# Prompt attention: the value products of a pair of heads in two column tiles of 64, in batches of two query tiles

## The reference, cut to what matters

```python
o_c = jnp.einsum("bqghc,bcgd->bqghd", p_c.astype(vc.dtype), vc)      # compressed keys
...
o_s = jnp.einsum("bqghm,bqgmd->bqghd", p_s.astype(v_sel.dtype), ...)  # selected blocks
...
o_w = jnp.einsum("bqghw,bwgd->bqghd", p_w.astype(vw.dtype), vw)       # window
...
o = g[..., 0, :] * o_c + g[..., 1, :] * o_s + g[..., 2, :] * o_w
return o.reshape(b, nq, D_ATTN).astype(q.dtype)
```

## Time and profile before

| | before |
|---|---|
| median of 3 runs | 1059.06 us (1058.37 to 1059.9) |
| profiled execution, its own time | 1058.09 us |
| its span, first to last instruction | 1056.0 us |
| TensorE busy | 986.1 us, 93% of the span |
| VectorE busy | 649.7 us, 62% |
| ScalarE busy | 404.6 us, 38% |
| GpSimd busy | 386.6 us, 37% |

### The profile page before, as it was taken

How to read it: one execution, slowest core, us unless ns; L and a number is a source line. 1 busy time by engine, 2 the same in 40 slices (tenths; PEclk the granted TensorE clock), 3 DMA queues, 4 the chain that set the end, 5 groups by cost and what they waited for, 6 DMA issues and landing times.

```text
span 1056.0 us, 19270 instructions
## 1 busy us (share of the span) xinstructions
PE 986.1 (93%) x7168; PEld 836.4 (79%) x7168; DVE 649.7 (62%) x1399; ACT 404.6 (38%) x794; POOL 386.6 (37%) x328
## 2 busy tenths in 40 slices
PE   2999999999999959999899998999699999999996
PEld 0989998998899729998799678999577777756684
DVE  4498999899989679320751312344888888833103
ACT  5333334333334276221331111244577777711001
POOL 2487888788878658001010000000333333100000
PEclk9999999999999959999899999998799999999796
DMA  8243453355334450360255015211630000260002
GB/s 342 75 128 101 127 174 103 101 139 163 101 105 137 139 202 1 120 238 7 115 152 133 1 26 221 80 61 41 205 124 1 0 1 1 104 235 1 1 1 85
DMA packets 43016, 108.01 MB, mean 102 GB/s; under 512 B 20674, under 2 KB 21730, under 8 KB 38530
## 3 DMA queue, kind: packets, MB, share of 16 engines
q1 hardware_dynamic: 42946, 106.99, 31.2%
HBM read 81.87 MB, written 12.17 MB: 89 GB/s over the span
## 4 chain that ended last, share of the span: by engine, by line
PE 82%; DVE 7%; issue 4%; ACT 4%; POOL 3%; DMA 0%; DVEq 0%; ACTq 0%
PE ps L567 52%; PE ps L953 7%; PE ps L593 4%; PE ps L843 4%; POOL C L1737 3%; PE ps L731 2%; PE ps L831 2%; PE ps L939 1%; PE ps L545 1%; DVE SX L1527 1%; DVE KL L1496 1%; PE ps L820 1%; PE ps L795 1%; DVE X L1263 1%; PE ps L822 1%
## 5 line engine op out<-in xcount | busy, mean ns | idle before, releaser
L567 PE MATMUL ps<-Hh,ringAh 128*128 128x256 f32 (+1 forms) x768 | 161.2, 291 | 14.3 <-DVE X L1263 14.3
L567 PE MATMUL ps<-Hh,ringAl 128*128 128x256 f32 (+1 forms) x768 | 159.4, 289 | 0.0
L1307 DVE SCALAR_TENSOR_TENSOR acc<-VP,tapc,acc 128x512 f32<-128x512 f32 x122 | 159.1, 1304 | 0.0
L567 PE MATMUL ps<-Xl,ringAh 128*128 128x256 f32 (+1 forms) x768 | 158.1, 287 | 0.0
L1706 POOL TENSOR_TENSOR ringAl<-ringA,ringAh 128x1024 fp32r<-128x1024 f32 x48 | 121.1, 2535 | 73.3 <-ACT ringAh L1029 73.2
L567 PEld LDWEIGHTS ps<-Hh,ringAh 128*128 128x128 f32 x768 | 123.3, 189 | 27.2 <-DVE X L1263 14.6
L567 PEld LDWEIGHTS ps<-Xl,ringAh 128*128 128x128 f32 x768 | 124.1, 189 | 0.0
L567 PEld LDWEIGHTS ps<-Hh,ringAl 128*128 128x128 f32 x768 | 123.0, 189 | 0.0
L1307 DVE SCALAR_TENSOR_TENSOR ps<-VP,tapc,ps 128x512 f32<-128x512 f32 x138 | 102.8, 745 | 0.6
L843 PE MATMUL ps<-PTB,V 128*128 128x512 f32 (+3 forms) x256 | 91.0, 439 | 2.5 <-ACT PTB L1206 2.1
L567 PE MATMUL ps<-Hh,ringEh 128*128 128x256 f32 (+1 forms) x384 | 84.2, 302 | 7.1 <-DVE ringEl L1373 4.6
(11 more groups left out here) (233 smaller groups left out, 2059.6 us busy)
## 6 DMA issues: line engine op xcount, KB each, us to landing
ringA<-in_w_a SPq DMA_DIRECT2D x16, 1536.0 KB, 7.3
G<-VP SPq DMA_DIRECT2D x60, 260.0 KB, 4.8
ringE<-in_w_f SPq DMA_DIRECT2D x24, 512.0 KB, 3.6
ringC<-in_w_c SPq DMA_DIRECT2D x8, 1024.0 KB, 5.9
cache_cmp<-in_cache_cmp SPq DMA_DIRECT2D x32, 128.0 KB, 2.8
cache_sel<-in_cache_sel SPq DMA_DIRECT2D x16, 256.0 KB, 3.0
cache_win<-in_cache_win SPq DMA_DIRECT2D x1, 4096.0 KB, 15.2
out_win_s<-in_win_state SPq DMA_DIRECT2D x1, 4032.0 KB, 18.1
```

What stands on the lines that cost most here:

```text
L567: mm = nc.tensor.matmul(dst, w, x[:, cols], start=begins, stop=ends)
L1307: nc.vector.scalar_tensor_tensor(tap_sum(k % 2), src, w, tap_sum(k % 2), ALU.mult, ALU.add).then_inc(conv_step, 1)
```

## The change

The order of a step's units becomes: branch b, then early (t = 0, 1) or late (t = 2, 3) query tiles, then head r, then t. So four units in a row hold both heads' weights for two query tiles of one branch. After units 1, 5, 9 and 13 TensorE issues a batch `pv(i, m)` for four such units: for each key tile the products of both heads in turn, each with 64 columns of `V` as the stationary operand, head 0 into rows 0 to 63 and head 1 into rows 64 to 127 of one bank, which alternates with the step. The product of the compressed branch is issued once per step, ahead of the first batch. The transposed weights lie in two tiles, `PTA` for early and `PTB` for late query tiles. The gate product is one instruction over 128 rows. The queries `QS` exist twice and are made a step earlier; the bias is made after the last score that uses the old one. TensorE's loop over steps is written out; VectorE's and GpSimd's loops take two steps in a turn.

```diff
+def unit(u):
+
+    m = u // 4
+    return u % 4 // 2, m // 2, 2 * (m % 2) + u % 2
...
-        QS = [at("QS0", [P, NP_], NR - 2048, F32R), at("QS1", [P, NP_], PTR + NP_ * 4, F32R)]
-        PTB = at("PTB", [P, 2, 4, NP_], HR)
+        QS = [[at("QS00", [P, NP_], NR - 2048, F32R), at("QS01", [P, NP_], PTR + NP_ * 4, F32R)],
+              [at("QS10", [P, NP_], SMT + 2 * P * 4, F32R), at("QS11", [P, NP_], NR + 4 * (NKEY + P) * 4, F32R)]]
+        PTA = at("PTA", [P, 2, 2, 2, 2, P], HR)
+        PTB = at("PTB", [P, 2, 4, 2, P], HR + 8 * 2 * P * 4)
...
-            def pv(i, n, gp):
...
-                mm = nc.tensor.matmul(out[:, P * k:NP_], V[:, k, v:v + P], PTB[:, b, k, P * k:NP_],
-                                      start=False, stop=(b == 1 and k == 3))
...
+            def pv(i, m):
+
+                gp, b, late = i // 4, m // 2, m % 2
+                bank = 6 + i % 2
+                if m == 0:
+                    if i == 0:
+                        pe.wait_ge(cs_kept, 4)
+                        pe.wait_ge(pt_zeroed, 1)
+                    if i >= 2:
+                        pe.wait_ge(og, i - 1)
+                    pe.wait_ge(pc_set, i + 1)
+                    nc.tensor.matmul(ps[:, bank], vcd[:, gp, :], PT[:, 0, :], start=True, stop=False)
+                pe.wait_ge(pt_kept, 16 * i + 4 * m + 4)
+                for k in range(2 + 2 * late):
+                    first = max(k, 2 * late)
+                    for r in range(2):
+                        v = b * GROUPS * HD + gp * P + HD * r
+                        src = (PTB[:, r, k] if late else PTA[:, b, r, k])[:, first % 2:2, :]
+                        mm = nc.tensor.matmul(ps[HD * r:HD * r + HD, bank, P * first:P * (2 + 2 * late)], V[:, k, v:v + HD],
+                                              src.rearrange("p t q -> p (t q)"), start=False, stop=(b == late == 1 and k == 3))
+                mm.then_inc(pv_done, 1)
+
+            for i in range(8):
                 for u in range(16):
                     if u >= 4:
                         transpose(i, u - 4)
-                    elif reaches(i, 1):
+                    elif i >= 1:
                         transpose(i - 1, u + 12)
...
+                    qk(i, u, i // 4)
+                    if u % 4 == 1:
+                        if u >= 8:
+                            pv(i, u // 4 - 2)
+                        elif i >= 1:
+                            pv(i - 1, u // 4 + 2)
+            for u in range(4):
+                transpose(7, u + 12)
+            pv(7, 2)
+            pv(7, 3)
...
-            def gate_head(i, r):
...
+            def gate_heads(i, par):
+
+                dve.wait_ge(pv_done, 4 * i + 4)
+                nc.vector.tensor_tensor(ZT[:, i, 0:NP_], ps[:, 6 + par], ZT[:, i, 0:NP_], ALU.mult).then_inc(og, 1)
...
-                    if u == 5 and reaches(i, 1):
-                        gate_head(i - 1, 0)
-                    if u == 13 and reaches(i, 1):
-                        gate_head(i - 1, 1)
...
+                    if u == 7 and reaches(i, 1):
+                        gate_heads(i - 1, 1 - par)
...
+            def distance(i, r):
                 if reaches(i, 1):
-                    pool.wait_ge(sc_ready, 16 * i + 8 * r - 8)
+                    pool.wait_ge(sc_ready, 16 * i - 2 + 2 * r)
...
+            def step(i, par):
+                query(i, par, 0)
+                if not reaches(i, 1):
+                    distance(i, 0)
+                query(i, par, 1)
+                if not reaches(i, 1):
+                    distance(i, 1)
                 compressed(i)
...
+                if reaches(i, 1):
+                    distance(i, 0)
+                    distance(i, 1)
```

More of the change, by code:

```diff
@@ L810, in qk @@
             def qk(i, u, gp):
-                r, b, t = u // 8, u % 8 // 4, u % 4
+                r, b, t = unit(u)
                 n = (t + 1) * P
-                if u % 8 == 0:
+                q = QS[i % 2][r][:, t * P:(t + 1) * P]
+                if u < 4 and u % 2 == 0:
                     pe.wait_ge(ql_set, 2 * i + r + 1)
-                if u % 4 == 0 and not reaches(i, 1):
+                if u % 8 == 0 and i == 0:
                     pe.wait_ge(kl_ready, 4 * b + 4)
-                if u >= 4 or reaches(i, 1):
+                if u >= 4 or i >= 1:
                     pe.wait_ge(sc_ready, 16 * i + u - 3)
[L820 to L823, removed]
+                nc.tensor.matmul(ps[:, u % 4, 0:n], q, KS[b][:, 2 * gp + r, 0:n], start=True, stop=False)
+                nc.tensor.matmul(ps[:, u % 4, 0:n], q, KL[r][:, b, gp, 0:n], start=False, stop=True).then_inc(qk_done, 1)
             def transpose(i, u):
-                t = u % 4
+                t = unit(u)[2]
                 pe.wait_ge(p_ready, 16 * i + u + 1)
-                if u >= 2 or reaches(i, 1):
+                if u >= 2 or i >= 1:
                     pe.wait_ge(pt_kept, 16 * i + u - 1)
@@ L966, in _ @@
                 if v == 0:
-                    pe.wait_ge(og, 16)
+                    pe.wait_ge(og, 8)
                 if quarter == 0:
@@ L1193, in exp @@
             def exp(i, u):
-                n = (u % 4 + 1) * P
+                n = (unit(u)[2] + 1) * P
                 act.wait_ge(sc_ready, 16 * i + u + 1)
@@ L1200, in copy_weights @@
             def copy_weights(i, u):
-                turn, t = u // 4 % 2, u % 4
+                r, b, t = unit(u)
                 act.wait_ge(t_done, 16 * i + u + 1)
[L1204 to L1207, removed]
+                if u == 4 and reaches(i, 1):
+                    act.wait_ge(pv_done, 4 * i)
+                elif u == 12:
+                    act.wait_ge(pv_done, 4 * i + 2)
+                elif u % 8 == 0 and reaches(i, 1):
+                    act.wait_ge(pv_done, 4 * i - 3 + 2 * b)
+                dst = PTA[:, b, r, 0:t + 1, t % 2, :] if t < 2 else PTB[:, r, 0:t + 1, t % 2, :]
+                nc.scalar.activation(dst, ps[:, 4 + u % 2, 0:(t + 1) * P].rearrange("p (k q) -> p k q", q=P),
                                      ACT.Copy).then_inc(pt_kept, 1)
@@ L1502, in score @@
             def score(i, u):
-                r, n = u // 8, (u % 4 + 1) * P
-                if u % 8 == 0:
+                r, b, t = unit(u)
+                n = (t + 1) * P
+                if u < 4 and u % 2 == 0:
                     dve.wait_ge(bias_set, 2 * i + r + 1)
@@ L1554, in attend @@
                         set_gates(i)
-                    if u == 5 and reaches(i, 1):
-                        gate_head(i - 1, 0)
-                    if u == 13 and reaches(i, 1):
-                        gate_head(i - 1, 1)
-            attend(0)
-            with dve.Fori(1, 8) as i:
-                attend(i)
+                    if u == 7 and reaches(i, 1):
+                        gate_heads(i - 1, 1 - par)
+            attend(0, 0)
+            attend(1, 1)
+            with dve.Fori(1, 4) as j:
+                attend(2 * j, 0)
+                attend(2 * j + 1, 1)
             normalize(7, 14)
@@ L1565, in _ @@
             normalize(7, 15)
-            gate_head(7, 0)
-            gate_head(7, 1)
+            gate_heads(7, 1)
             dve.wait_ge(sbias_in, 16)
@@ L1796, in compressed @@
                 nc.gpsimd.tensor_copy(PT[0:HD, 0, :], PCT[:, i, :]).then_inc(pc_set, 1)
-            def step(i):
-                head(i, 0)
-                head(i, 1)
-                compressed(i)
-            step(0)
-            with pool.Fori(1, 8) as i:
-                step(i)
+                pool.wait_ge(pc_set, i + 1)
+            def step(i, par):
[5 more added lines that the diff above has]
+                    distance(i, 1)
+                compressed(i)
+                if reaches(i, 1):
+                    distance(i, 0)
+                    distance(i, 1)
+            step(0, 0)
+            step(1, 1)
+            with pool.Fori(1, 4) as j:
+                step(2 * j, 0)
+                step(2 * j + 1, 1)
 def feature_major(xp, xs):
```

35 lines of the change are left out of this document (10 added, 25 removed).

## The result

The changed kernel takes 1068.72 us (median of 20 runs, 1060.34 to 1075.14), the one before 1058.95 us (median of 20) beside it: a ratio of 1.0066, with an interval of 1.004 to 1.0091. It is slower, by about 7 us by the ratio and 10 by the medians. The 20 runs of the kernel before lie in two groups, 12 around 1058 us and 8 around 1067; the ratio is that of the means, and the median lies in the faster group. The profiled execution took 1067.67 us, its span 1065.9.

The account below looks back on a forecast made before the run. TensorE was taken as the bound at 21.0 us a step, VectorE close behind. Batches and round trips of 19.7 plus GpSimd's 0.2 make 19.9; seven steps save 7.7: 1059.1 - 7.7 = 1051.4, say 1051 us, range 1037 to 1061.

Parts of the forecast that it names:

- Side by side: TensorE's value products: both heads run at once in two column tiles, 4.32 us a step where 8.64 stood.
- Change of form: TensorE switching between full-width array and tiles around each batch: 0.13 us each way, 1.04 us a step.
- Batches and round trips: TensorE-VectorE path: batches of 6.27 us plus four round trips, 2 x 3.69 and 2 x 3.02, 19.7 us a step.
- GpSimd: GpSimd's subtractions holding up VectorE's normalizations early in a step: between 0 and 1.4 us a step, 0.2 taken.
- The clock: Rival: TensorE, idle in short pieces, drops to half clock once a step, giving 1063 us; chance 0.07.
- theory 1: Formed after the measurement: GpSimd's bunched work holds up VectorE on the batches' way, and TensorE, starved, loses its clock.
- The start: First step: queries also meet the subtractions for the low part of the keys; no size given, left in the range.
- the round trip eats it: Rival: 0.28 us more per round trip, from blocked normalizations or late exponentials, cancels the gain; 1057 to 1062 us, chance 0.17.

Follow-up runs that it names:

- experiment 4: The retimed kernel with both heads' value products in one column tile, except the last pair of a step: 1080.35 us (one run).
- experiments 1, 2: Changed kernel: GpSimd's queries cut to one column from the third step, 1056.99 us; biases too, 1056.71; second experiment: the retimed kernel, 1047.84.
- retimed kernel: Changed kernel with GpSimd's query work waiting for the step before's scores of unit 5 (first head) and 9 (second): 1047.84 us, ratio 0.9905.
- two with small groups: Changed kernel with its batches split into smaller groups of products behind more units, GpSimd's query work left in place: 1055.64 us, ratio 0.9949.
- experiment 5: Changed kernel with GpSimd's query subtraction made a copy from the third step, 1053.73 us; or subtraction and bias product in four pieces, 1050.54 us.
- the one with six groups: The retimed kernel with value products in six groups a step, early batches whole and late ones in two halves: 1042.55 us, ratio 0.983.

## Why the prediction was wrong

- **Side by side: right.** 4.32 us a step; undone, it costs 4.1 (experiment 4).
- **Change of form: right to 0.02.** 0.15 us each way on the path, where 0.13 was taken.
- **Batches and round trips: right, and not by errors that cancel.** From the end of a batch to the start of the next the retimed kernel takes 3.12, 3.71, 3.26 and 3.95 us (828.90 to 832.02, 833.68 to 837.39, 838.19 to 841.45, 843.11 to 847.06), where the round trips of 3.02 and 3.69 with one change of form make 3.15 and 3.82. 19.7 us a step was the sum without GpSimd; 19.73 and 19.74 were measured (experiments 1, 2), in the changed kernel itself in its last step, which makes no queries. The retimed version's attention ends 7.6 us earlier than before, where 7.7 were forecast.
- **GpSimd: the step that failed.** "Between 0 and 1.4 us; I take 0.2, since most fall into VectorE's idle time." It is 2.0 us a step at full clock (21.71 - 19.73), above both of these bounds. I counted two normalizations held by 0.7 and looked at GpSimd's work by its amount; but the wait that the change gives the queries is already met when the second bias is finished, so all of it runs in one piece at a step's start, where VectorE's idle time isn't. And I named the copy of the gates but put no wait on it: 0.18 us of work that waits 1.1 us and has the normalization of unit 0 behind it.
- **The clock: a rival that I gave a chance of 0.07 by itself, and that came only with the step above.** The three steps of the chain with the fall in the late batch take 1.6 to 2.1 us more than the 21.71 of the one that has only the holds. Only the kernels with both whole subtractions at a step's start show it (four stretches in the changed kernel, two with small groups, none from 774 to 906 us in the others). The retimed kernel runs the same transposes, scores and tiles at 1.00, so none of these brings it about by itself; by the page that I had cited (TensorE: Matmul & The Clock Gate, Part 4, of the Trainium skill) the transposes alone could have. What makes it fall stays open: TensorE's waits stand ahead of each of the four falls in the changed kernel, but the step from 882.98 has the same two waits, 1.31 and 0.98 us, with TensorE busy for 1.46 of 3.4 us, and keeps 1.00. So theory 1 holds for the holds on VectorE, and its second half, that starvation lets the clock fall, is not shown.
- **The start.** The first L852 of the chain is at 812.20 and in the retimed version at 807.57; 4.6 us are lost there; for the first step I had left the meetings with the subtractions to the range. One step with the holds and a stretch at half clock (804) lies in it, 3.9 at the price of the next ones.

The sum from these: 4.6 + (23.77 + 23.28 + 23.73 - 3 x 19.74) + (21.71 - 19.74) = 18.1 us, against 18.05 by which the sequences' scores of the changed kernel (939.50) lie behind those of the retimed one (921.45). So the forecast's tiles and round trips were right, and the rival "the round trip eats it", named with its cause, came true with 2.0 us a step in place of 1.4; the clock's 1.6 to 2.1 in four stretches came on top, and took the time past the range.

## What to carry to other kernels

When work is moved off one path, look at what it runs beside in its new place: an operation's price for its neighbours is set by when it runs. GpSimd's waits are worth as much care as its amount: tie them to a moment at which VectorE has run dry, and cut long operations into pieces where that can't be had. When TensorE's work is cut on a path that then runs through a second engine, look for what that engine could be held up by, tiny operations included, since those stalls were covered before.

## What the runs showed of the hardware

A GpSimd copy or cast with one input held VectorE's copies and normalizations as a subtraction did: they ended 0.03 to 0.08 us behind it (experiment 5, and the normalization of 848.75 in the changed kernel). But a normalization of 512 columns that met a cast only in its first 0.25 us (846.66 to 847.20 in the changed kernel, the cast until 846.91) kept its 0.54 us.

The clock of the final part, which no version changes, differs between executions and can hide what the attention gained. These are the windows from 964 to 988 us of the retimed kernel and of the one with six groups, both inside the output projection:

```profile
964.00:988.00 24.00, 24.00 (x98) 16.48 (x99) 5.15 (x20) 0.00 (x0) 0.00 (x0) 0.75 0.00 1
```
```profile
964.00:988.00 24.00, 24.00 (x70) 16.61 (x69) 3.62 (x12) 0.00 (x0) 0.00 (x0) 0.56 0.00 0
```

TensorE is busy throughout in both, at a granted clock of 0.75 and of 0.56. From the first of the sequences' scores to the end it is 124.9 us in the first (921.45 to 1046.3) and 132.4 in the second (911.25 to 1043.6), so only 2.7 of the 10.2 us gained in the attention show in these two executions. Why the clock goes down under dense work there was not tried and stays open.
